# First layer's shift and scale by columns of 8, 4 and 4 k blocks, the first three tiles projected k block by k block between the loads

## The reference

```python
mod = jax.nn.silu(c) @ w_ada + b_ada
shift, scale, gate = jnp.split(mod, 3, axis=-1)
h = _rmsnorm(x, g_norm) * (1.0 + scale[:, None, :]) + shift[:, None, :]
cols = jnp.split(h @ w_in, np.cumsum(COL_SIZES)[:-1].tolist(), axis=-1)
...
y = x + gate[:, None, :] * (o @ w_out)
```

## Time and profile before

| | us |
|---|---|
| median of 3 runs | 2387.77 (2385.23 to 2389.59) |
| profiled execution | 2384.53 |
| its span | 2382.7 |
| TensorE busy | 2321.0 (97%) |
| GpSimd busy | 933.7 (39%) |
| VectorE busy | 1299.2 (55%) |
| ScalarE busy | 753.9 (32%) |

### The profile page before, as it was taken

How to read it: one execution, slowest core, us unless ns; L and a number is a source line. 1 busy time by engine, 2 the same in 40 slices (tenths; PEclk the granted TensorE clock), 3 DMA queues, 4 the chain that set the end, 5 groups by cost and what they waited for, 6 DMA issues and landing times.

```text
span 2382.7 us, 49827 instructions
## 1 busy us (share of the span) xinstructions
PE 2321.0 (97%) x20956; PEld 2166.8 (91%) x20956; DVE 1299.2 (55%) x2526; ACT 753.9 (32%) x1215; POOL 933.7 (39%) x668
## 2 busy tenths in 40 slices
PE   6699999999999999999998999999999999999998
PEld 3399999999999999988888999999999999999998
DVE  4355666677776333452227566666777743344444
ACT  2242232333334333331114323233333333334111
POOL 0143333444333433463334344343334433346542
PEclk8799999999999999999999999999999999999999
DMA  9952333544455444368875333344544445444343
GB/s 390 343 185 74 95 94 95 150 127 127 127 146 138 129 139 131 108 188 262 248 227 182 86 91 90 92 136 131 140 134 127 123 125 143 137 123 117 107 115 109
DMA packets 467336, 347.19 MB, mean 146 GB/s; under 512 B 18701, under 2 KB 417513, under 8 KB 463745
## 3 DMA queue, kind: packets, MB, share of 16 engines
q1 hardware_dynamic: 467114, 344.02, 49.2%
HBM read 312.07 MB, written 32.09 MB: 144 GB/s over the span
## 4 chain that ended last, share of the span: by engine, by line
PE 83%; DVE 6%; DMA 4%; DVEq 2%; POOL 1%; ACT 1%; SPq 1%; issue 1%; ACTq 0%; POOLq 0%
PE pj L673 66%; PE mx L679 3%; DMA rows<-in_w_ada 2%; DVE t L1449 2%; PE mx L961 2%; POOL wlo L641 1%; PE mx L987 1%; PE mx L772 1%; PE mx L796 1%; PE mx L975 1%; DVE dt L1443 1%; PE pj L1085 1%; PE mx L939 1%; PE mx L989 1%; PE mx L979 1%
## 5 line engine op out<-in xcount | busy, mean ns | idle before, releaser
L673 PE MATMUL pj<-hh,whi 128*128 128x260 f32 x4960 | 1433.0, 289 | 9.2 <-DVE hl L1449 8.1
L641 POOL TENSOR_TENSOR wlo<-raw,whi 128x512 fp32r<-128x512 f32 x632 | 888.8, 1437 | 1331.0 <-ACT whi L1163 1331.0
L673 PE MATMUL pj<-hl,whi 128*128 128x260 f32 x4960 | 1401.9, 283 | 0.0
L673 PE MATMUL pj<-hh,wlo 128*128 128x260 f32 x4960 | 1401.5, 283 | 0.0
L673 PEld LDWEIGHTS pj<-hh,whi 128*128 128x128 f32 x4960 | 935.4, 189 | 72.0 <-issue 65.5
L673 PEld LDWEIGHTS pj<-hl,whi 128*128 128x128 f32 x4960 | 936.1, 189 | 0.0
L673 PEld LDWEIGHTS pj<-hh,wlo 128*128 128x128 f32 x4960 | 934.8, 188 | 0.0
L1163 ACT ACTIVATE whi<-raw 128x2048 fp32r<-128x2048 f32 x158 | 302.8, 1916 | 253.3 <-PE pj L673 218.3
L1163 ACT ACTIVATE xv<-pj 128x260 f32<-128x260 f32 x188 | 64.9, 384 | 412.4 <-PE pj L673 412.1
L1449 DVE SCALAR_TENSOR_TENSOR o<-pj,mod,t 128x260 f32<-128x260 f32 (+1 forms) x56 | 24.6, 480 | 233.0 <-PE pj L673 217.0
L1163 ACT ACTIVATE t<-t 128x520 f32<-128x520 f32 (+1 forms) x125 | 78.9, 631 | 171.9 <-DVEq L1694 125.0
(11 more groups left out here) (285 smaller groups left out, 2284.6 us busy)
## 6 DMA issues: line engine op xcount, KB each, us to landing
raw<-in_w_in SPq DMA_DIRECT2D x256, 512.0 KB, 5.3
raw<-in_w_out SPq DMA_DIRECT2D x64, 512.0 KB, 5.7
rows<-in_w_ada SPq DMA_DIRECT2D x26, 1024.0 KB, 14.0
lev<-in_w_ada SPq DMA_DIRECT2D x39, 512.0 KB, 4.9
out<-ss SPq DMA_DIRECT2D x32, 512.0 KB
lev<-in_w_ada SPq DMA_DIRECT2D x64, 256.0 KB, 5.4
gate_b<-in_w_ada SPq DMA_DIRECT2D x64, 256.0 KB, 4.8
xv<-in_w_ada SPq DMA_DIRECT2D x25, 512.0 KB, 4.9
```

The lines of the kernel that those rows point to most:

```text
L641: last = e.tensor_tensor(wlo[:, par, cs], w[:, cs], high_of(t)[:, cs].bitcast(F32), ALU.subtract)
L673: last = e.matmul(pj[:, 2 * par + b, 0:HALF], w[:, par, kb * P:(kb + 1) * P], x[:, kb, b * HALF:(b + 1) * HALF], start=(kb == 0 and m == 0 ...
```

## The change

The pieces are cut otherwise. The columns of shift and scale are loaded in three blocks of k blocks (`FIRST_BLOCKS`): 8, 4 and 4, each first shift, then scale. Pieces 0 to 7 are shift of k blocks 0 to 7, pieces 8 to 15 their scale, with two row blocks of 1024 columns each; pieces 16 to 31 are shift and scale of k blocks 8 to 11 and 12 to 15, four to a part, with four row blocks of 512 columns each. Two more places take pieces (`xv` and `spare_piece`, the latter in memory of `hc` and others), and the third tile has its own low part `wlo_third`, in the memory of `ss`. Tiles 0 and 1 are loaded behind piece 9, tile 2 behind piece 17. TensorE projects k blocks 0 to 9 of all three tiles with the pieces 17 to 29 in between, then the other k blocks of tiles 0 and 1, then those of tile 2. The fourth tile is projected in three passes (`by_pass`), with `scores` and `rows` behind k block 7 of the first pass, `states_u` behind k block 3 of the third, `outputs` in the fifth tile. `fetch(0)` waits for the third tile. Layer 1 keeps its order, but for two small memsets of VectorE that now stand behind the k blocks.

```diff
-        piece_slot = [0, 1, 2, 3, 4, 5, 10, 11, 6, 7, 8, 9, 10, 11, 6, 7, 8, 9, 10, 11, 6, 7, 8, 9, 10, 11, 8, 9, 10, 11, 8, 9]
+        piece_at += [xv[:, 0:D], spare_t[:]]
+        piece_slot = [0, 1, 2, 3, 4, 5, 10, 11, 12, 13, 6, 7, 8, 9, 10, 11, 12, 13, 8, 9, 10, 11, 12, 13, 9, 11, 12, 13, 9, 11, 12, 13]
...
+        def piece_of(piece):
+
+            if piece < 16:
+                return 0, piece // 8, piece % 8, 2
+            return 1 + (piece - 16) // 8, piece // 4 % 2, piece % 4, 4
+
+        def column_block(u):
+
+            first, count = FIRST_BLOCKS[u // 2]
+            pieces = 8 * (u + 1) if u < 2 else 16 + 4 * (u - 1)
+            return first, count, count * P // 4, pieces
...
-                if p == 17:
+                if p == 9:
                     e.wait_ge(piece_used, 2)
                     first_tiles(0)
+                if p == 17:
+                    load(2, 0, w_in[0].rearrange("(k p) n -> p k n", p=P)[:, :, COLS[KINDS[0]][2]:COLS[KINDS[0]][2] + HD])
...
-                fetch(0)
                 if l == 0:
                     e.wait_ge(lm_taken, 1)
                 else:
+                    fetch(0)
                     e.wait_ge(ada_used, ADA_GROUPS * ADA_PIECES)
...
                     if h == 0:
                         if l == 0:
-                            e.wait_ge(xt_taken, KB)
-                            e.wait_ge(sct_taken, 1)
+                            e.wait_ge(tile_done, 3)
+                            fetch(0)
...
-                if t % TILES == 2:
+                if t == TILES + 2:
                     e.wait_ge(tile_done, t - 1)
...
                 tile_wait(t0, 0, l * NH)
                 tile_wait(t0 + 1, 1, l * NH)
...
+                if l == 0:
+                    e.wait_ge(lo_done, 3)
+                    e.wait_ge(rs_made, 1)
+                    for kb in range(10):
+                        pair_block(kb)
+                        third_block(kb)
+                        for p in ((17,), (18,), (19,), (20,), (21,), (22, 23), (), (24, 25), (26, 27), (28, 29))[kb]:
+                            first_piece(p)
+                        if kb == 4:
+                            block_columns(2)
+                        if kb == 6:
+                            block_columns(3)
+                    block_columns(4)
+                    first_piece(30)
+                    first_piece(31)
+                    pair_block(10)
+                    block_columns(5)
+                    for kb in range(11, KB):
+                        last = pair_block(kb)
...
+                if l == 0:
+                    for kb in range(10, KB):
+                        last = third_block(kb)
+                    last.then_inc(tile_done, 1)
...
+                        if g == 0:
+                            return ({}, {}, {(0, 7): (scores, rows), (2, 3): (states_u,)}), {0: (outputs,), 5: (back,)}
...
                 if l == 0:
+                    block_take(0)
                     e.wait_ge(prm_tr, 1)
                     params(1)
-                    norm(0)
-                    block_take(0)
                     for j in range(2):
                         high(j, 1, j, False)
+                    norm(0)
+                    high(2, 2, 0, False)
                     block_take(1)
...
                             if h or j > 1:
                                 high(t + 2, (t + 2) // 2 + 1, j % 2)
-                            elif j == 0:
-                                high(t + 3, (t + 3) // 2 + 1, 1)
+                            elif j == (0 if l else 1):
+                                high(t0 + 3, (t0 + 3) // 2 + 1, 1)
```

More of the change, by code:

```diff
@@ L730, in first_piece @@
                 def first_piece(p):
+                    block, which, i, ks = piece_of(p)
+                    u = 2 * block + which
+                    n, pieces = column_block(u)[2:]
                     e.wait_ge(piece_in[piece_slot[p]], 16 * (loads_of(p) + 1))
-                    at = piece_at[piece_slot[p]]
-                    if p < KB:
-                        w = at.rearrange("p (c j n) -> p j c n", j=4, n=P)
+                    if i == 0 and u >= 2:
+                        e.wait_ge(mod_made, u - 1)
@@ L736, in first_piece @@
+                    for x in range(ks):
+                        w = piece_at[piece_slot[p]].rearrange("p (k c j n) -> p k j c n", k=ks, j=4, n=P)[:, x]
                         for j in range(4):
[L737 to L749, removed]
@@ L750, in first_piece @@
-                    last.then_inc(piece_used, 1)
[L752 to L760, removed]
+                            last = e.matmul(mx[32 * j:32 * j + 32, 2 + which, 0:n].rearrange("p (c n) -> p c n", n=P),
+                                            sct[:, ks * i + x, :], w[:, j], start=(i == 0 and x == 0), stop=(p == pieces - 1 and x == ks - 1))
@@ L761, in block_columns @@
+                    last.then_inc(piece_used, 1)
+                def block_columns(u):
+                    e.wait_ge(block_taken, u + 1)
+                    for c in range(0, column_block(u)[2], P):
+                        last = tr(mx[:, 2 + u % 2, c:c + P], (qd, dt)[u % 2][:, c:c + P], P)
                     last.then_inc(block_tr, 1)
@@ L841, in third, with third_block, by_pass @@
                     last.then_inc(tile_done, 1)
+                def third_block(kb):
+                    for b in range(2):
+                        for m, (w, x) in enumerate(((whi_third, hh), (wlo_third, hh), (whi_third, hl))):
+                            last = e.matmul(mx[:, b, 0:HALF], w[:, kb * P:(kb + 1) * P], x[:, kb, b * HALF:(b + 1) * HALF],
+                                            start=(kb == 0 and m == 0), stop=(kb == KB - 1 and m == 2))
+                    return last
+                def by_pass(t, par, hooks):
+                    e.wait_ge(hi_done, t + 1)
+                    e.wait_ge(taken, 4)
+                    for m, (w, x) in enumerate(((whi, hh), (whi, hl), (wlo, hh))):
+                        if m == 2:
+                            e.wait_ge(lo_done, t + 1)
+                        for kb in range(KB):
+                            for b in range(2):
+                                last = e.matmul(pj[:, 2 * par + b, 0:HALF], w[:, par, kb * P:(kb + 1) * P],
+                                                x[:, kb, b * HALF:(b + 1) * HALF],
+                                                start=(kb == 0 and m == 0), stop=(kb == KB - 1 and m == 2))
+                            if (m, kb) == (2, KB - 1):
+                                last.then_inc(tile_done, 1)
+                            for hook in hooks.get((m, kb), ()):
+                                hook()
@@ L1047, in _ @@
                             own[j][part] = own[j].get(part, ()) + (lambda x=x: gate_session(h, x),)
-                    if h == 0:
+                    if h == 0 and l:
                         third(t + 2, g)
-                    for j in range(1 if h else 3, 4):
-                        tile(t, j, g, own[j - 1])
+                    if g == 0:
+                        by_pass(t + 3, 1, own[2])
+                    else:
+                        for j in range(1 if h else 3, 4):
+                            tile(t, j, g, own[j - 1])
                     if h + 1 < NH:
```

118 lines of the change are left out of this document (62 added, 56 removed).

## The result

| | before | after |
|---|---|---|
| median, beside each other on one chip | 2386.5 (2383.7 to 2389.6) | 2419.8 (2413.9 to 2420.9) |
| ratio | | 1.0133 (95%: 1.0121 to 1.0146) |
| span of the profiled execution | 2382.7 | 2419.1 |
| TensorE busy | 2321.0 | 2327.7 |

The change costs 33 us; I had forecast 19.5 and a range that ended at 2415. Direction and both waits of 8 us were right, the size was not.

A forecast was written before the change was run, and what follows sets the result against it. TensorE bounds all but the transfer-bound start, whose losses carry to the end. TensorE resuming 17.8 us later plus 1.7 for the lower clock gave 19.5 on 2387.8, so 2407, range 2396 to 2415.

The forecast's parts named there:

- both waits of 8 us: TensorE idle some 8 us at the scores (head's constants late) and again at the row transposes (fifth tile's weights late).
- S: First projection matmul: forecast at 83.9 us, 12 us earlier than before, behind the third tile's cast and the second block's copy.
- X: End of the third tile: forecast at 141.9 us, when it used to end at 141.8.
- The chain: VectorE's operations from the add to the first projection matmul: 6.5 us taken, between ends of 4.1 and 7.9.
- the quiet row: Profile row of the kernel before, where VectorE's chain took 4.1 us with GpSimd quiet.
- From S to the last piece: Ten k blocks, thirteen pieces, transposes and a slow start, 38.2 us together, with TensorE setting the pace over the loads.
- the gate row: Gate projection's matmuls over 130 columns, 28 ns each, 0.90 us a piece; basis for taking 0.95 us a piece.
- the 62.5 ns rival: Pieces' matmuls take 62.5 ns each, fifteen pieces cost 16 us more, time 2423; chance 5%.
- From X on: Fourth tile, scores, then row transposes at 164.3 us, held by the fifth tile's load behind y_kept and state.
- The queue lets small loads through: Rival: y_kept doesn't hold the fifth tile, so only the scores' wait is left; time 2399; chance 12%.
- An earlier S: Rival: third tile's weights come sooner or the copy doesn't wait; S = 75, all behind it 9 us earlier, 2398; 9%.
- The overlap pays: Rival: ScalarE's in-order casts cost nothing and constants are there in time; fourth tile 7 us earlier, 2381; chance 7%.

The follow-up runs named there:

- A: The changed kernel again, unedited, on another chip, against the kernel before: median 2413.2 us, ratio 1.0122.
- F: Changed kernel with pieces 17 to 21 used ahead of the projection and the rest earlier in the loop: 2398.9 us, ratio to the kernel before 1.0064.
- E: Kernel before, with only the first head's state and constants and the store of y_kept moved behind the third tile: 2402.7 us, ratio 1.0078.
- C: Changed kernel with the head's constants (hc) fetched before the wait for the third tile: 2412.2 us, ratio to the kernel before 1.0116.
- B: Changed kernel with y_kept stored before the wait for the third tile: 2405.2 us, ratio to the kernel before 1.0083.
- K: J with the third tile loaded, cast and projected later and only pieces 16 and 17 used ahead: 2377.5 us, ratio to the kernel before 0.9969.
- J: H with the fifth tile's load issued first, ahead of the constants and the y_kept store: 2380.8 us, ratio to the kernel before 0.9981.
- H: F with y_kept stored and the head's constants fetched before the wait for the third tile: 2387.9 us, ratio to the kernel before 1.0016.

## Why the prediction was right and wrong

| gate | forecast | after | A |
|---|---|---|---|
| third tile's cast | 74.4 | 77.2 | 76.0 |
| S, first projection matmul | 83.9 | 87.2 | 86.1 |
| last piece starts | 123.1 | 130.6 | 129.7 |
| pair block 12 | 130.3 | 139.6 | 136.4 |
| X (SP's first fetch behind it) | 141.9 | 151.5 | 148.3 |
| fourth tile starts | 144.4 | 153.2 | 150.0 |
| rotation starts | 147.0 | 156.5 | 153.5 |
| scores | 154.5 | 162.8 | 159.7 |
| fifth tile's cast | 161.9 | 172.6 | 169.4 |

*S: right in kind, 3.3 us short (A: 2.2).* The order of ScalarE did what the fence said. The chain was 7.1 for 6.5; the rest is the weights' arrival. The Trainium skill's lock between VectorE and GpSimd ("SBUF — State Buffer", "Who interferes with whom") had it at some 8 by my estimate, and this trace agrees better with the rule than with the quiet row: `ag` took 1.28 us beside GpSimd and 0.23 without it. Three of the chain's operations were long, not each. The row I gave for the rule is weaker than I made it: GpSimd was at work beside both multiplies of the earlier trace rows (its subtractions ran from 129.71 to 135.70 without a break), and only the second took 1.80.

*From S to the last piece: the step that failed.* I wrote that "here TensorE sets the pace, and the loads wait for it", from 3.3 us per k block and piece against 2.6 of transfer. Both numbers were right: a k block and piece took 3.36 (from 92.54 to 95.89), and a piece of 32 records 1.08 at full clock, so the gate row was the right one (I had 0.95) and the 62.5 ns rival is out. What the sum left out is when the loads may go out. The plan uses one piece per k block at first and two later, and of the first five used only three give back a place that is taken again: one transfer could start per two k blocks, so 87 to 108 us ran at 137 GB/s. When two are wanted each k block, 4.2 us, two transfers of 2.7 to 3 don't fit in it. Pieces 29, 30 and 31 were waited for (0.6, 1.4, 1.7; in A 1.0, 1.6, 1.6). In the first profile piece 31 and the pair block behind it also ran at a granted clock of 0.50; in A piece 31 didn't. From S to the last piece I had 39.2 us and it took 43.4 (A: 43.6), and from S to X 58.0 against 64.2 (A: 62.2). F shows it from the other side: the order of use changed, with ScalarE's copies to suit, and 14 us came back. I had compared the two rates and not walked the places.

*From X on: right.* From X to the start of the row transposes I had 22.1 us and it took 23.3 (151.45 to 174.73); E, with nothing but this tail, measured 19.0 for the 17 to 19 expected. The prediction tells of two waits of some 8 us, but its sum goes by the gate that comes last, the fifth tile's cast, and doesn't add them. C bears that out: taking the first wait away gives nothing.

*The rivals.* "The queue lets small loads through" is out: the fifth tile landed behind y_kept, and B, which takes y_kept away, gains. "An earlier S" was given 9 us of gain; K has an S earlier still (74.3) and gains 3.3 on J, with other edits in it. "The overlap pays" was not this kernel, yet J and K are what it would take: the weights and constants there when their turn comes.

*The total.* Against the forecast, A's profile has +28.6 for 19.5: 2.2 at S, 4.2 more by X, 1.1 more in the tail, the rest behind it. The first profile had another 3.7 in layer 1 that A's had not. The forecast of 2407 was 6 below A and 13 below the first median, and the range closed 5 us below that median: it held no term for loads that can't catch up. A's 2413.2 lies inside the range, but that is luck: the same loads stood still there (141 GB/s).

## What to carry to other kernels

When work is woven into a stream of loads through a ring of places, don't compare mean rates; walk the ring: for each load, whose use gives back its place, when that is, and how many loads are in flight when the consumer starts to take two at a time. A use whose place no later load takes starts no transfer. Use up what has landed during idle time, even if nobody needs its result yet, because it frees the place. And when two waits stand in a row on one engine, and the second doesn't hang on the first, the gate that comes last sets the price of both: moving the other one only hands its time over (C).

## What the runs showed of the hardware

- Rows of 2 KB ran at 385 to 387 GB/s in a full queue, 4 KB at 410, 8 KB at 416. The same 2 KB rows came at 340 to 343 with four places in turn (108 to 123 us, A and the first profile).
- The granted clock can be lost after a short gap. Before the fourth tile TensorE stands for 1.75 us in H, J and K alike, and the 16 matmuls behind it took 3.63 us in H (granted clock 0.54), 3.04 in J (0.69) and 2.19 in K (1.00). What it takes for one gap to cost the clock and another not, these runs don't tell.
- SP itself can be the one that waits: in the changed kernel, behind y_kept and the next head's state, its issue of half a tile at 153.44 took 10.6 us; y_kept landed at 166.4.
- The same program took 3.7 us longer in layer 1 in one profile than in another: a difference of this size between two single profiles has to be placed on the time axis before it is explained.
